# The root mean square of the feed-forward blocks: sums with tokens on partitions, and a row made by a diagonal's product

## The reference

```python
def rmsnorm(x, g):
    x32 = x.astype(jnp.float32)
    y = x32 * lax.rsqrt(jnp.mean(x32 * x32, axis=-1, keepdims=True) + EPS)
    return (y * g.astype(jnp.float32)).astype(x.dtype)

def swiglu(h, w_in, w_out):
    gate, up = jnp.split(h @ w_in, 2, axis=-1)
    return (jax.nn.silu(gate) * up) @ w_out

x = x + 0.5 * swiglu(rmsnorm(x, norm_g[layer, 0]), ffn_w_in[layer, 0], ffn_w_out[layer, 0])
```

## Time and profile before

| | |
|---|---|
| median of three executions | 2118.66 us (2115.07 to 2119.27) |
| the profiled execution | 2114.99 us, its span 2113.2 us |
| TensorE busy | 2044.1 us, 97% of the span |
| VectorE, ScalarE busy | 1464.0 us (69%), 1114.7 us (53%) |
| the sums, L735 | 64 passes in four blocks, the starts of the blocks' first and last 15.6 and 957.2 us |
| mean granted clock of TensorE | 0.996 |

### The profile page before, as it was taken

The page is one execution under the profiler, slowest core; times in us unless marked ns, Lnnn a source line. Parts: engine busy times, 40 slices in busy tenths (PEclk is TensorE's granted clock), DMA queues, the critical chain, the costliest instruction groups (busy, mean ns, idle before and its releaser), DMA issues. The chain is left out here.

```text
span 2113.2 us, 34585 instructions
## 1 busy us (share of the span) xinstructions
PE 2044.1 (97%) x14050; PEld 1853.5 (88%) x14050; DVE 1464.0 (69%) x2157; ACT 1114.7 (53%) x1580; POOL 26.3 (1%) x35
## 2 busy tenths in 40 slices
PE   7999999999999999989999989999999889999998
PEld 7999997999999998879999967888888758888886
DVE  5666785666666665576665477788987466888896
ACT  4333733544343445574333456677775455776774
POOL 1000000000000020000000000000000000000000
PEclk9999999999999999999999999999999999999999
DMA  9555322655545543435553532589985514789992
GB/s 310 186 186 184 123 89 92 211 185 186 186 148 185 185 146 100 154 124 189 186 184 124 156 123 100 204 323 368 351 328 207 220 40 160 271 328 337 343 359 93
DMA packets 246671, 421.44 MB, mean 199 GB/s; under 512 B 7716, under 2 KB 135104, under 8 KB 246432
## 3 DMA queue, kind: packets, MB, share of 16 engines
q1 hardware_dynamic: 245632, 418.09, 56.2%
q0 software_dynamic: 544, 1.62, 0.2%
q10 hardware_dynamic: 384, 0.21, 0.1%
HBM read 416.70 MB, written 1.05 MB: 198 GB/s over the span
## 5 line engine op out<-in xcount | busy, mean ns | idle before, releaser
L662 PE MATMUL banks<-x_hi,w_hi 128*128 128x256 f32 x1360 | 385.8, 284 | 0.0
L663 PE MATMUL banks<-x_lo,w_hi 128*128 128x256 f32 x1360 | 384.9, 283 | 0.0
L664 PE MATMUL banks<-x_hi,w_lo 128*128 128x256 f32 x1360 | 384.8, 283 | 0.0
L3318 DVE TENSOR_TENSOR w_lo<-weight_ring,w_hi 128x1024 fp32r<-128x1024 f32 x256 | 300.3, 1220 | 25.4 <-ACT w_hi L3136 16.9
L608 ACT ACTIVATE w_hi<-weight_ring 128x1024 fp32r<-128x1024 f32 x87 | 92.0, 1057 | 419.3 <-PE banks L664 419.2
L624 DVE TENSOR_TENSOR w_lo<-weight_ring,w_hi 128x1024 fp32r<-128x1024 f32 x88 | 107.7, 1224 | 242.4 <-ACT w_hi L608 242.4
L3136 ACT ACTIVATE w_hi<-weight_ring 128x1024 fp32r<-128x1024 f32 x256 | 256.0, 1053 | 36.0 <-PE banks L2966 20.4
L1084 DVE TENSOR_TENSOR pieces<-weight_ring,pieces 128x512 fp32r<-128x512 f32 (+2 forms) x245 | 167.8, 692 | 144.4 <-ACT pieces L1073 141.9
L662 PEld LDWEIGHTS banks<-x_hi,w_hi 128*128 128x128 f32 x1360 | 261.1, 192 | 0.2
L663 PEld LDWEIGHTS banks<-x_lo,w_hi 128*128 128x128 f32 x1360 | 261.1, 192 | 0.1
L664 PEld LDWEIGHTS banks<-x_hi,w_lo 128*128 128x128 f32 x1360 | 261.1, 192 | 0.0
(11 more groups left out here) (406 smaller groups left out, 4079.8 us busy)
## 6 DMA issues: line engine op xcount, KB each, us to landing
weight_ring<-in_ffn_w_in SPq DMA_DIRECT2D x88, 1024.0 KB, 7.6
weight_ring<-in_moe_w_gate SPq DMA_DIRECT2D x64, 1024.0 KB, 6.6
weight_ring<-in_moe_w_up SPq DMA_DIRECT2D x64, 1024.0 KB, 9.0
weight_ring<-in_moe_w_down SPq DMA_DIRECT2D x48, 1024.0 KB, 11.9
weight_ring<-in_ffn_w_out SPq DMA_DIRECT2D x44, 1024.0 KB, 9.8
weight_ring<-in_moe_w_down SPq DMA_DIRECT2D x8, 2048.0 KB, 11.5
weight_ring<-in_hg_w_in SPq DMA_DIRECT2D x12, 1024.0 KB, 8.2
weight_ring<-in_fox_w_in SPq DMA_DIRECT2D x12, 1024.0 KB, 8.4
```

Of the source, the lines that this page charges most:

```text
L662: pe.matmul(out, w_hi, m_hi, start=start, stop=False, skip_group_check=True)
L663: pe.matmul(out, w_hi, m_lo, start=False, stop=False, skip_group_check=True)
L664: return pe.matmul(out, w_lo, m_hi, start=False, stop=stop, skip_group_check=True)
L3318: dve.tensor_tensor(self.gate_up_piece(s, p, self.w_lo), self.gate_up_piece(s, p), self.gate_up_piece(s, p, self.w_hi.bitcast(F32)), ALU.s ...
```

## The change

The sums are made with the squares stationary and one column of ones streaming. A product then gives the sum of 128 tokens on 128 partitions, one column for each half of the tokens, two in all, in a corner of the same PSUM bank. ScalarE's root and VectorE's reciprocal work on 128 x 2 values in the new tile `norm_cols`. To get back the row that every partition needs, VectorE multiplies the identity by each of the two columns (two diagonal matrices in `std`, `norm_diag`), and TensorE multiplies ones by these (`pe_rows`): every row of the result is the diagonal. That product stands inside step 1's gate/up, behind 21 of its 48 passes. ScalarE copies the result from PSUM to `rstd` (`act_row`), and VectorE waits for that ahead of its step loop. Step 1's gate/up is taken out of TensorE's loop, whose body now has down ahead of gate/up.

```diff
+    def pe_second(self, pe):
+        k = self.k
+        pe.wait_ge(k.gu_lo, self.j0 + 2)
+        pe.wait_ge(k.h_ready, self.j0 + 2)
+        for part in range(2):
+            for kk in range(KD):
+                last = self.pe_half(pe, 1, part, kk)
+                if part == 0 and kk == 6:
+                    self.pe_rows(pe)
+        last.then_inc(k.gu_ready, 1)
+
+    def pe_rows(self, pe):
+        k, out = self.k, self.ring_bank(2)
+        pe.wait_ge(k.norm_diag, 2 * self.ffn + 2)
+        for t in range(TT):
+            last = pe.matmul(out[:, t * P:(t + 1) * P], k.ones, k.std[:, t * P:(t + 1) * P], start=True, stop=True, skip_group_check=True)
+        last.then_inc(k.norm_row, 1)
...
     def pe_sums(self, pe):
-        k, out = self.k, self.ring_bank(2)[:, 0:T]
+        k, out = self.k, self.ring_bank(2)[:, T:T + TT]
         for kk in range(KD):
             if kk % 2 == 0:
                 pe.wait_ge(k.norm_sq, 4 * self.norm + kk // 2 + 1)
-            last = pe.matmul(out, k.ones, k.sq[:, kk], start=kk == 0, stop=kk == KD - 1)
+            for t in range(TT):
+                last = pe.matmul(out[:, t:t + 1], k.sq[:, kk, t * P:(t + 1) * P], k.ones[:, 0:1], start=kk == 0 and t == 0,
+                                 stop=kk == KD - 1, skip_group_check=True)
         last.then_inc(k.norm_sum, 1)
...
-        turns, rest = divmod(self.steps - 1, 2)
+        self.pe_second(pe)
+        turns = (self.steps - 2) // 2
         with pe.Fori(0, turns) as i:
             for t in range(2):
-                self.pe_gate_up(pe, (t + 1) % 2, i * 2 + (self.j0 + t + 1))
-                self.pe_down(pe, t % 2, i * 2 + (self.j0 + t))
-        for j in range(2 * turns, self.steps - 1):
-            self.pe_gate_up(pe, (j + 1) % 2, self.j0 + j + 1)
-            self.pe_down(pe, j % 2, self.j0 + j)
-        pe.wait_ge(k.norm_std, self.ffn + 1)
+                self.pe_down(pe, t, i * 2 + (self.j0 + t))
+                self.pe_gate_up(pe, t, i * 2 + (self.j0 + t + 2))
+        self.pe_down(pe, (self.steps - 2) % 2, self.j0 + self.steps - 2)
+        pe.wait_ge(k.norm_row_read, self.ffn + 1)
...
-        act.activation(k.std[:], self.ring_bank(2)[:, 0:T], ACT.Sqrt, bias=k.const(C_EPS, 1), scale=1.0 / D).then_inc(k.norm_std, 1)
+        act.activation(k.norm_cols[:, 0:TT], self.ring_bank(2)[:, T:T + TT], ACT.Sqrt, bias=k.const(C_EPS, 1), scale=1.0 / D).then_inc(k.norm_std, 1)
+
+    def act_row(self, act):
+        k = self.k
+        act.wait_ge(k.norm_row, self.ffn + 1)
+        act.activation(k.rstd[:], self.ring_bank(2)[:, 0:T], ACT.Copy).then_inc(k.norm_row_read, 1)
...
             self.act_split(act, 1, self.j0 + 1, 0)
+        self.act_row(act)
         with act.Fori(0, self.turns) as i:
...
-        dve.reciprocal(k.rstd[:], k.std[:]).then_inc(k.norm_rstd, 1)
+        dve.reciprocal(k.norm_cols[:, TT:2 * TT], k.norm_cols[:, 0:TT]).then_inc(k.norm_rstd, 1)
         dve.wait_ge(k.norm_rstd, self.norm + 1)
+        for t in range(TT):
+            dve.tensor_scalar(k.std[:, t * P:(t + 1) * P], k.ident, k.norm_cols[:, TT + t:TT + t + 1], None, ALU.mult).then_inc(k.norm_diag, 1)
...
             self.dve_split_gu(dve, 1, self.j0 + 1)
+        dve.wait_ge(k.norm_row_read, self.ffn + 1)
         with dve.Fori(0, self.turns) as i:
```

More of the change, by code:

```diff
@@ L265, in __init__ @@
         self.norm_sum, self.norm_std, self.out_done = s("norm_sum"), s("norm_std"), s("out_done")
+        self.norm_diag, self.norm_row, self.norm_row_read = s("norm_diag"), s("norm_row"), s("norm_row_read")
+        self.norm_cols = f32("norm_cols", [P, 2 * TT])
         self.piece_hi, self.piece_lo, self.piece_used = s("piece_hi"), s("piece_lo"), s("piece_used")
```

## The result

The changed kernel takes 2131.95 us in the median of 10 executions (2123.8 to 2138.06), the kernel before, run in turn with it on the same chip, 2118.86 us (10 executions, 2115.05 to 2122.96). The ratio is 1.0063, with a 95% interval of 1.0046 to 1.0081: slower by 13.1 us, between 10 and 17. The forecast was 2128 us, in a range of 2122 to 2134.

A forecast was written before the change was run, and what follows sets the result against it. The prediction took TensorE, busy 97% of the span, as the bound. Chain and row 4.8, falls of the clock 3.0 and the first block's late rise 3.0 made +10.8 us on 2117.0: 2128 us, range 2122 to 2134.

The forecast's parts named there:

- The sums: Products of sums on TensorE: 32 one-column passes at 0.107 us replace 16 wide ones, +0.1 us a block (0 to +0.15).
- Faster: Rival, 4%: one-column passes in the sums do not cost their load; at most -8 us, 2109 us.
- The row and the chain: Step 1's path through root, reciprocal, row and h_lo to the down product: 1.2 us later a block, +4.8 us (3.6 to 6).
- S: The start of step 1 in a block, from which the forecast counts its times in us.
- The table load: SiLU's table load on ScalarE, 1.28 us, now behind the copy: 0.35 us of cover left, costed at nothing.
- The clock in the later blocks: TensorE's clock falls to half speed behind the sums in two of three later blocks: +3.0 us (0 to 9).
- more of the clock: Rival, 20%: the clock falls in each of three blocks, some for twice the length; 2131 to 2134 us.
- my forecast: The prediction's own case, 53%: chain and row, two clock falls and a slower first block; 2128 us, own range 2125 to 2131.
- The first block: First block: chain and row 1.1 to 1.2 us, and a late rise from half speed +3.0 us (0 if unmoved).
- The sum: All terms over the whole kernel: 4.8 + 3.0 + 3.0 = +10.8 us.
- the prediction's price: Cost of one clock fall, from 16 passes at 860 us: 3.41 us against 1.92 at full level, 1.5 us.

The follow-up runs named there:

- the first experiment: The changed kernel with the products of sums streaming 128 columns of ones in place of one: 2117.52 us, ratio 0.999 to the kernel before.
- the early row: The row's product behind 12 of step 1's passes, not 21, in the changed kernel: 2125.51 us with 128 columns streamed in the sums, 2125.09 us with one.
- after: The changed kernel, with one-column sums and the row behind 21 passes, against the kernel before: 2131.95 us, ratio 1.0063.
- late row: The row's product behind 21 of step 1's passes, as in the changed kernel: 2131.95 us with one column streamed in the sums, 2117.52 us with 128.
- the last experiments: Dense zero products added to the kernel before (2125.32, 2119.47 us), the changed kernel with 128-column sums (2128.17 us) and the kernel before with folded squares (2117.18, 2117.75 us).
- the folded kernel: The kernel before, with VectorE adding the upper four squares to the lower four in the later blocks, so TensorE sums 8 passes, not 16: 2116.41 us.

## Why the prediction was right, by its steps

**The sums: right in kind, a little short.** 3.27 to 3.49 us a block is +0.22 where I took +0.1, outside its bounds of 0 to 0.15; the pace is 0.109. The Trainium skill, TensorE: Matmul & The Clock Gate, Back-to-back issue gap, has a floor of about 25 ns for a product of 1 to 64 columns. The measurement shows that this floor is not what such products cost when each brings 128 new stationary float32 columns: one, 32, 64 and 128 columns all ran at 0.11 us a pass. The rival *Faster* died with that.

**The row and the chain: right, in size too.** This is read from the first experiment, where no fall disturbs it. Row at S + 2.59 (forecast 2.6), diagonal ready more than 1 us earlier, block +1.2 us without a fall, as three blocks of the first experiment show. Parts were off and cancelled: the copy took 0.38 us where I took 0.47, and VectorE's gap ahead of the multiplication was 0.22 as forecast, so it came at S + 3.84 and not S + 4.0; the sums took 0.1 more. The row's four passes cost 0.33 us (step 1 with the early row takes 6.27 us, before 5.94), under the forecast's 0.46 and its lower bound of 0.43; TensorE waits for the chain anyway, so the sum does not feel it. TensorE's idle time was 0.49 us, forecast 0.6. The experiment with the early row shows this idle time is the chain's: with the row 9 passes earlier it is gone. The table load stayed hidden: in after's third block SiLU ends at 605.43 and hidden starts at 605.73, 0.30 us of cover, forecast 0.35.

**The clock in the later blocks: mechanism right, size too small.** This is the mis-sized term. I took two falls of 1.5 us, +3.0; there were three, one of double length, 3.1 + 1.5 + 1.5 = 6.1 us. The rows that I weighed pulled apart, 1.7 us of such passes without a fall and 3.7 us with one (the "3.4 us and more" of the forecast stood in no row); with 3.5 us the profiled kernels show 8 falls in 9 blocks. One of these rows was weak: around 361 the clock fell while TensorE stood idle for 1.83 us (358 to 359 reads 0.71 with no pass in it), so of the two rows behind passes over few partitions only the one at 860 shows a fall without an idle time. The rival "more of the clock" described these blocks better than my forecast did, and the median, 2131.95, lies in its 2131 to 2134 and not in the 2125 to 2131 of my own forecast. Its condition, that the passes be slowed themselves, held in the second block, where the clock fell during the sums. The rule from the Trainium skill, TensorE: Matmul & The Clock Gate, section Why this matters for your kernels, to leave no idle gaps between bursts, would have given no fall. Here the engine had no gap in any of those microseconds, and changing the streamed columns alone, at equal pace and equal busy time, took the falls away. The rule alone did not protect this kernel.

**The first block: near.** +3.6 us, forecast 1.2 + 3.0 = 4.2. The mechanism shows in the timeline of TensorE in after:

```profile
15.44 6.99 PE L758 MATMUL banks<-consts,squares 128*128 128x1 f32 x32 [0.94 <-DVEq L191]
22.29 0.56 PE L664 MATMUL banks<-x_hi,w_hi 128*128 128x256 f32 x1
...
23.07 0.41 PE L664 MATMUL banks<-x_hi,w_hi 128*128 128x256 f32 x1
...
37.43 0.39 PE L664 MATMUL banks<-h_hi,w_hi 128*128 128x256 f32 x1 [0.49 <-DVE h_lo L657]
```

All 32 passes run at 0.21 us, the gate/up passes behind them go on at that pace until 26 us, and in the earlier trace rows the turn came before 21.35. Each kernel has one profile, and the moment of the turn scatters among them, but not without order. In five of the fourteen (four of them with 128 or 256 columns) the passes were at full pace by 15.2 us, before the sums. In the six others with 128 or 256 columns the turn came between 18.8 and 21.1 us, in the three others with 1, 32 or 64 columns at 26.0, 27.4 and 27.5 us. The first blocks of the latter took 22.0 to 22.7 us, those with the same late row and 128 columns 19.65 and 18.85. With 64 columns the delay also shows in the rest of 13 executions, as said. Timeline of TensorE with 64 columns:

```profile
15.43 7.09 PE L759 MATMUL banks<-consts,squares 128*128 128x64 f32 x32 [0.94 <-DVEq L191]
...
27.33 0.37 PE L666 MATMUL banks<-x_hi,w_lo 128*128 128x256 f32 x1
27.54 0.28 PE L664 MATMUL banks<-x_hi,w_hi 128*128 128x256 f32 x1
```

The fifth early one is the kernel with one column and the early row. Its clock was up when the sums began, and then fell behind them, a fall that the count of the later blocks leaves out:

```profile
16.00:17.00 1.00, 1.00 (x11) 1.00 1.12 353
19.00:20.00 1.00, 1.00 (x6) 0.50 1.14 360
```

So the narrow sums delay the rise, by about what was forecast; how much of after's +3.6 us is this in the mean of many executions stays open.

**The sum.** +13.3 us in the blocks of the profiled execution against +10.8, and +13.1 in the median. That 13.3 and 13.1 agree is in part luck: the profiled execution lost another 9.7 us outside the blocks, and was one of the slowest. So is it in part that the time fell into the range: the forecast says nothing of losses outside the blocks, and these alone moved the medians of other kernels here by up to 10 us.

## What to carry to other kernels

A pass's cost in time and what the clock does behind it are two things. Here, where the stationary load set the pace, streaming 128 columns in place of one left the sums' time as it was and no fall came behind them in 9 blocks, against 8 falls in 9 with one column. So try a wider moving side for a long run of narrow products before counting what fewer columns save. But judge it in the stretch itself: with the late row the ratio went from 1.0063 to 0.999, with the early row the median did not move. And measure a change of a few microseconds by the part it touches, with busy time and clock apart, since the clock's losses in distant stages differed by up to 10 us between kernels that differ here by a few microseconds of work.

## What the runs showed of the hardware that was not expected

**The clock's losses outside the blocks change with small edits elsewhere.** 1.7 us of zero products in the first block cost 10.65 us; 5.1 us of them in four places cost nothing; the early row, by which the rest sank by 5.1 us, cost 8 us; 4.4 us less work in the later blocks brought no gain that can be told. In each case the rest moved in the direction of the work, within 2 us of it, and the loss did not. The clock fell at 861 us in one of two kernels that issue the same passes there, and the fall at 860 us on which the prediction's price rests was absent from the kernel with 128 columns. That the place of the stages in time decides it was the idea behind the last experiments, and it is not shown: the added products moved the stages by other amounts than their own length, the loss of the folded kernel only went from 19.8 to 16.05, and I have one profiled execution of each kernel. Therefore the 9.7 us outside after's blocks can't be put down to the one-column sums themselves, and of the 14 us between one and 128 columns only the three later blocks' 6.1 us, and the first block's 2.3 in the profiled executions, are shown pass by pass.

**At the program's start the granted clock does not tell the pace.** It reads 1.00 in the first stretches while products run at the paces of half speed (0.21 us for a pass of load and one column in after, against 0.109 later). There the pace of passes must be read, not the clock.
